# The two halves of a product bank taken in turn, matmul by matmul, in every chunk of a two-layer block

## The chip, the core and the metric

The kernel runs on one core of one Trainium2 chip. The metric is the device time in microseconds of one execution; it stands as the median of several executions. TensorE is PE in the profile (its weight loads are PEld), VectorE is DVE, ScalarE is ACT, GpSimd is POOL, SyncE is SP.

## The reference

A two-layer block on 256 tokens of width 1024, all in float32. What matters here are its large products; each is `activations @ weights`:

```
z = h @ w_in                                   # values va, vb among the columns
merged = sum_b sigmoid(zg_b + b_gate_b) * (y_b @ w_branch[b])      # 3 branches, 256 -> 1024
y = merged @ w_out
a, g = split(h @ w_up);  y = (gelu(conv(a)) * g) @ w_down          # 1024 -> 2816 -> 1024
q, k, v, g, a_lr = split(x @ gla_w_in);  y = (...) @ gla_w_out     # second layer, gated linear attention
k, v = split(x @ w_kv);  q, gate = x @ swa_w_in;  y = (...) @ swa_w_out
```

Between them stand norms, three kinds of attention over 256 tokens, a chunked linear attention and a dilated window attention.

## The kernel before

**Products in three parts.** Every float32 operand is split into a high part in a faster matmul format (`whi`, `hhi`) and the rest (`wlo`, `hlo`). A product of a 128x128 block of weights with 256 columns is then three matmuls: high by high, low by high, high by low. `three` (lines 1596 to 1598) issues them one after the other into one place in PSUM.

**Chunks.** The weights are cut into 106 chunks, mostly 1024 rows by 256 columns, that run in a fixed order: the input projection (MISC, QA, KA, VA, QB, KB, VB, then twelve gate chunks from ZG), three BRANCH chunks, four WOUT, 22 UP, twelve DOWN, the second layer's GK to GG, GOUT, SK, SV, sixteen SWA, SOUT. SP loads each chunk into one of four `raw` buffers, ACT writes `whi` from it (line 639, `high`), DVE writes `wlo` (line 1052, `low`), each in one of three slots. A slot is free when the chunk three before has been multiplied. The order of ACT's and DVE's instructions is written out by hand: in turn c, with b = c - 1, ACT first splits chunk c + 2 and then drains the result of chunk b.

**Results.** A full chunk fills a PSUM bank of 128x512: 256 columns for the first 128 outputs (half i = 0) and 256 for the next (i = 1). There are three result banks, `res0` to `res2`, used in turn. `bank(r)` makes PE wait, ahead of the next matmul that it issues, until result r - 3 is drained. `product_done` counts finished products; ACT and DVE wait for it.

**How the halves are taken before.** A plain chunk of `fm` already takes its halves in turn (`both_sides`, matmuls on line 1631). A chunk that is broken by attention work ("units", `parts`, `half`), or that waits for its input piece by piece (`ready`), does half i = 0 over all eight k and then half i = 1. So do `fm_first` (for each k the three matmuls of a half, then those of the next), `tm` (VA, VB, GV to GV+3, SV to SV+2: tokens as the stationary side, values as result) and the branch projection.

**The down projection.** A pair of output blocks j takes three chunks, kg = 0, 1, 2 with 8, 8 and 6 blocks k, 132 matmuls in all. Its two halves go to two different banks, results r = 2j and r + 1 of this stage. Within each chunk half 0 runs over all its k, then half 1. ACT drains both (lines 863 and 866: the square, then the scaled copy whose end frees the bank); in that turn it has first split chunk b + 3, which takes the slot of the chunk whose end it drains, and so waits for that end:

```python
for i in range(2):
    ps = bank(r + i) if kg == 0 else res[(r + i) % NB]
```

```python
if DOWN <= b < GK and (b - DOWN) % 3 == 2:
    j = (b - DOWN) // 3
    for i in range(2):
        ps = result(FIRST_RESULT[b] + i)
        nc.scalar.activation(sq[:, 2 * j + i, :], ps[:, 0:T], ACT.Square).then_inc(squares["n4"], 1)
```

**Turned.** After the waits at the start of WOUT and UP, `turned` issues three matmuls with the activations as moving and stationary side exchanged into a place that nobody reads.

Of the kernel before, what the change touches and what calls it, by code (L numbers as in the profile page):

```python
# [18 lines left out]
D, T, P = 1024, 256, 128  # L19
KT = D // P  # L20
D_FF = 2816
FT = D_FF // P
# [3 lines left out]
RAW, SPL, NB = 4, 3, 3  # L26
# [12 lines left out]
QI, KK, QC, MISC, QA, KA, VA, QB, KB, VB = range(10)  # L39
# [171 lines left out]
def build(nc, xT, crow_d, cols_d, ident_d, rope1_d, rope2_d, amask_d, cmask_d, tri_d, dmask_d, sel_d, rel_d, w_a2_d,  # L211
# [4 lines left out]
    with ctx:  # L216
# [32 lines left out]
        with ExitStack() as st:  # L249
# [21 lines left out]
            yhi = sb("yhi", [P, 3, 512], f32r, at=st)  # L271
            ylo = sb("ylo", [P, 3, 512], f32r, at=st)
# [3 lines left out]
        w = sq[:, :, :].rearrange("p a b -> p (a b)").rearrange("p (t n) -> p t n", t=2)  # L276
# [19 lines left out]
        with ExitStack() as st:  # L296
            uhi = sb("uhi", [P, FT, T], f32r, at=st)
            ulo = sb("ulo", [P, FT, T], f32r, at=st)
# [50 lines left out]
        res = [ctx.enter_context(nc.psum_tensor(f"res{i}", [P, 512], f32)) for i in range(NB)]  # L349
# [9 lines left out]
        product_done, drained_act, drained_dve = sem("product_done"), sem("drained_act"), sem("drained_dve")  # L359
# [1231 lines left out]
        def _(pe):  # L1591
            mm = nc.tensor.matmul

            def three(out, ah, al, bh, bl, first, last):

                mm(out, ah, bh, start=first, stop=False)  # L1596
                mm(out, al, bh, start=False, stop=False)  # L1597
                return mm(out, ah, bl, start=False, stop=last)  # L1598

            def bank(r):  # L1600

                if r >= DIRECT + NB:
                    who, n = RESULT_DRAIN[r - NB]
                    pe.wait_ge(drained[who], n)
                return res[r % NB]
# [8 lines left out]
            def weights_of(c):  # L1614
                kt, w = kt_of(c)
                return tuple(h[:, 0:kt * w].rearrange("p (k n) -> p k n", k=kt) for h in halves(c))

            def half_product(c, i, k, ps, ih, il, at, first=None, last=None):

                wh, wl = weights_of(c)  # L1620
                return three(ps[:, i * T:i * T + T], wh[:, k, i * P:i * P + P], wl[:, k, i * P:i * P + P],
                             ih[:, k, :], il[:, k, :], at == 0 if first is None else first,
                             at == KT - 1 if last is None else last)

            def both_sides(c, ih, il, ps, order):

                wh, wl = weights_of(c)
                for at, k in enumerate(order):
                    for wt, ix, p in ((wh, ih, 0), (wl, ih, 1), (wh, il, 2)):
                        for i in range(2):  # L1630
                            last = mm(ps[:, i * T:i * T + T], wt[:, k, i * P:i * P + P], ix[:, k, :],  # L1631
                                      start=at == 0 and p == 0 and i == 0, stop=at == KT - 1 and p == 2 and i == 1)
                last.then_inc(product_done, 1)

            def fm(c, ih, il, half=None, ready=None, order=range(KT), parts={}):

                wait_weights(c)
                ps = bank(FIRST_RESULT[c])
                if not half and not ready and not parts:
                    both_sides(c, ih, il, ps, order)  # L1640
                    return
                for i in range(2):
                    for at, k in enumerate(order):
                        if ready and i == 0:
                            ready(k)
                        last = half_product(c, i, k, ps, ih, il, at)
                        if at == 7 and i:
                            last.then_inc(product_done, 1)
                        if at in (3, 7) and 2 * i + at // 4 + 1 in parts:
                            parts[2 * i + at // 4 + 1]()  # L1650
                    if i == 0 and half:
                        half()

            def warm(n, of=ident, to=pS[:, 512:640]):
# [9 lines left out]
            def fm_first(c, ih, il, ready, order=range(KT)):  # L1664


                wait_weights(c)
                wait_weights(c + 1)
                ps = bank(FIRST_RESULT[c]), bank(FIRST_RESULT[c + 1])
                for at, k in enumerate(order):  # L1670
                    ready(k)
                    for d in range(2):
                        for i in range(2):
                            last = half_product(c + d, i, k, ps[d], ih, il, at, i == 0 and at == 0, i == 1 and at == KT - 1)
                        if at == KT - 1:
                            last.then_inc(product_done, 1)

# [9 lines left out]
            def tm(c, ih, il):  # L1687

                wh, wl = weights(c)
                w = kt_of(c)[1]  # L1690
                ps = bank(FIRST_RESULT[c])
                for t in range(2):
                    if c == VB and t == 1:
                        forget_rows((2, 3))
                    for k in range(KT):
                        last = three(ps[:, t * 256:t * 256 + w], ih[:, k, t * P:t * P + P], il[:, k, t * P:t * P + P],
                                     wh[:, k, :], wl[:, k, :], k == 0, k == KT - 1)
                last.then_inc(product_done, 1)

            def in_low(n, k):  # L1700
# [173 lines left out]
            for c in range(DIRECT, NC):  # L1874
# [27 lines left out]
                elif c < WOUT:  # L1902
# [3 lines left out]
                        pe.wait_ge(y_lo, 3)  # L1906
                    for j in range(4):
                        ps = bank(FIRST_RESULT[c] + j)
                        for i in range(2):
                            n = 2 * j + i  # L1910
                            for k in range(2):
                                last = three(ps[:, i * T:i * T + T], wh[:, k, n * P:n * P + P], wl[:, k, n * P:n * P + P],
                                             yhi[:, b, k * T:k * T + T], ylo[:, b, k * T:k * T + T], k == 0, k == 1)
                        last.then_inc(product_done, 1)
                        if (b, j) in ((0, 1), (0, 3), (1, 1)):
                            units((24, 25, 26)[2 * b + j // 2])
# [26 lines left out]
                elif c < GK:  # L1943
# [1 line left out]
                    wh, wl = weights(c)  # L1945
                    kt = kt_of(c)[0]
                    r = 2 * j + FIRST_RESULT[DOWN]
                    for i in range(2):
                        ps = bank(r + i) if kg == 0 else res[(r + i) % NB]
                        for k in range(kt):  # L1950
                            kk = 8 * kg + k
                            if j == 0 and i == 0 and kk % 2 == 0:
                                pe.wait_ge(u_lo, kk // 2 + 1)
                            last = three(ps[:, 0:T], wh[:, k, i * P:i * P + P], wl[:, k, i * P:i * P + P],
                                         uhi[:, kk, :], ulo[:, kk, :], kk == 0, kk == FT - 1)
                        if i == 1 or kg == 2:
                            last.then_inc(product_done, 1)
                    if c == GK - 1:
                        sums("n4", stat)
                        last_squares("n4", stat)  # L1960
# [207 lines left out]
```

## Time and profile before

| | |
|---|---|
| median of 3 executions | 753.88 us |
| lowest, highest | 751.53, 757.02 us |
| the profiled execution | 751.74 us |
| its span, first to last instruction | 749.9 us |
| PE busy | 723.9 us, 5964 matmuls |
| DVE, ACT, POOL busy | 524.3, 395.7, 104.4 us |
| mean granted TensorE clock | 0.989 |

The profiled execution's time is 1.8 us more than its span, and 2.1 us less than the median. A row of a group gives the line, the engine, the instruction, output<-inputs, the number of instructions, and durations. A matmul's duration is modelled and runs past the start of the next, so the rate of PE is read from starts, not from durations.

### The profile page before, as it was taken

Reading aid. Unit: us, or ns where it says so; the run is one execution under the profiler, and the core shown is the slowest. Engines: PE = TensorE matmul, PEld = TensorE weight load, DVE = VectorE, ACT = ScalarE, POOL = GpSimd, SP = SyncE. Lnnn points to the kernel's source line nnn. Section 1 sums busy time; section 2 is a strip of 40 time slices with the busy share of each in tenths; the row PEclk is TensorE's granted clock in tenths of the full one; section 3 lists DMA queues with packets and bytes.
Section 4 is the critical chain, followed back from the end, with each engine's and each line's share of the span. In section 5 each row is a group of like instructions: output and inputs, shape, how many; then the busy total and the mean of one; then the engine's idle time right before and its main releaser. Section 6 shows DMA issues by size and latency. Waiting matters only on the chain.

```text
span 749.9 us, 14222 instructions
## 1 busy us (share of the span) xinstructions
PE 723.9 (97%) x5964; PEld 703.3 (94%) x5964; DVE 524.3 (70%) x778; ACT 395.7 (53%) x560; POOL 104.4 (14%) x87
## 2 busy tenths in 40 slices
PE   8999999998899999999999999999999999999995
PEld 6799899897898999999999989899999999999995
DVE  4979878886978687778776657836576356555665
ACT  4297455555354545544544348537554465556551
POOL 0030000000521000000000130000004465443000
PEclk9999999999999999999999999889999999999999
DMA  8995576566364456565567453604446654333101
GB/s 345 411 361 177 216 278 245 190 240 225 113 225 169 143 195 210 188 221 164 205 267 275 165 199 129 210 25 170 169 155 225 204 191 131 126 138 113 57 1 57
DMA packets 22265, 141.13 MB, mean 188 GB/s; under 512 B 2389, under 2 KB 3029, under 8 KB 6458
## 3 DMA queue, kind: packets, MB, share of 16 engines
q1 hardware_dynamic: 21626, 137.28, 50.4%
q0 software_dynamic: 576, 2.95, 1.0%
q8 instruction: 47, 0.77, 0.4%
q14 instruction: 16, 0.13, 0.0%
HBM read 139.17 MB, written 1.05 MB: 187 GB/s over the span
## 4 chain that ended last, share of the span: by engine, by line
PE 71%; DVE 13%; issue 7%; ACT 6%; DMA 2%; POOL 1%; DVEq 0%; ACTq 0%; POOLq 0%
PE res L1631 22%; PE res L1596 12%; PE res L1598 12%; PE res L1597 12%; ACT whi L639 4%; DVE wlo L1052 3%; PE pX L1816 2%; PE pX L1995 2%; PE pS L1796 1%; DMA shared<-in_w_ada 1%; DVE raw L1065 1%; PE pS L1657 1%; ACT sq L654 1%; DVE shared L1065 1%; PE pT L1806 1%
## 5 line engine op out<-in xcount | busy, mean ns | idle before, releaser
L1052 DVE TENSOR_TENSOR wlo<-raw,whi 128x2048 fp32r<-128x2048 f32 (+3 forms) x101 | 226.9, 2250 | 119.2 <-ACT whi L639 112.7
L639 ACT ACTIVATE whi<-raw 128x2048 fp32r<-128x2048 f32 (+3 forms) x101 | 188.2, 1865 | 102.0 <-issue 73.3
L1596 PE MATMUL res<-hhi,whi 128*128 128x256 f32 (+1 forms) x576 | 166.1, 288 | 4.1 <-DVE wlo L1052 1.5
L1597 PE MATMUL res<-hhi,wlo 128*128 128x256 f32 (+1 forms) x576 | 161.0, 280 | 0.0
L1598 PE MATMUL res<-hlo,whi 128*128 128x256 f32 (+1 forms) x576 | 161.0, 279 | 0.0
L1596 PEld LDWEIGHTS res<-hhi,whi 128*128 128x128 f32 (+1 forms) x576 | 107.5, 187 | 5.9 <-issue 3.4
L1597 PEld LDWEIGHTS res<-hhi,wlo 128*128 128x128 f32 (+1 forms) x576 | 107.5, 187 | 0.3
L1598 PEld LDWEIGHTS res<-hlo,whi 128*128 128x128 f32 (+1 forms) x576 | 107.2, 186 | 0.2
L1631 PE MATMUL res<-hhi,whi 128*128 128x256 f32 x544 | 106.8, 278 | 0.0
L1631 PE MATMUL res<-hlo,whi 128*128 128x256 f32 x544 | 106.4, 277 | 0.0
L1631 PE MATMUL res<-hhi,wlo 128*128 128x256 f32 x544 | 106.3, 277 | 0.0
L1631 PEld LDWEIGHTS res<-hhi,whi 128*128 128x128 f32 x544 | 82.3, 188 | 0.1
L1631 PEld LDWEIGHTS res<-hlo,whi 128*128 128x128 f32 x544 | 82.2, 188 | 0.0
L1631 PEld LDWEIGHTS res<-hhi,wlo 128*128 128x128 f32 x544 | 82.1, 188 | 0.0
L538 POOL TENSOR_TENSOR sq<-sq,rope 128x512 f32<-128x512 f32 x18 | 39.7, 2204 | 77.0 <-ACT sq L654 77.0
L1598 PE MATMUL res<-ulo,whi 128*128 128x256 f32 x176 | 48.6, 276 | 0.0
L1596 PE MATMUL res<-uhi,whi 128*128 128x256 f32 x176 | 48.6, 276 | 0.0
L1597 PE MATMUL res<-uhi,wlo 128*128 128x256 f32 x176 | 48.6, 276 | 0.0
L1065 DVE CUSTOM_DVE_ANT_0 raw<-raw,cact,cols 128x1024 f32<-128x1024 f32 x32 | 41.9, 1346 | 0.0
L1596 PE MATMUL res<-whi,hhi 128*128 128x256 f32 x144 | 40.4, 281 | 0.0
L1597 PE MATMUL res<-whi,hlo 128*128 128x256 f32 x144 | 40.0, 278 | 0.0
L1598 PE MATMUL res<-wlo,hhi 128*128 128x256 f32 x144 | 40.0, 278 | 0.0
(340 smaller groups left out, 1344.4 us busy)
## 6 DMA issues: line engine op xcount, KB each, us to landing
raw<-in_wts SPq DMA_DIRECT2D x97, 1024.0 KB, 4.9
raw<-in_w_ada SPq DMA_DIRECT2D x16, 1024.0 KB, 5.2
shared<-in_w_ada SPq DMA_DIRECT2D x6, 1024.0 KB, 11.0
gates<-in_wts SPq DMA_DIRECT2D x4, 768.0 KB, 13.1
raw<-in_wts SPq DMA_DIRECT2D x4, 768.0 KB, 6.0
y<-in_w_ada SPq DMA_DIRECT2D x2, 1024.0 KB, 9.3
x<-in_xT SPq DMA_DIRECT2D x2, 512.0 KB, 4.5
gv<-in_ln_rows POOLq DMA_DIRECT2D x1, 1024.0 KB, 7.4
```

Of the source, the lines that this page charges most:

```text
L538: nc.gpsimd.tensor_tensor(xsw, xsw, table[:, 1:2, :].to_broadcast([P, 2, T]), ALU.mult).then_inc(sin_done, 1)
L639: nc.scalar.activation(hi[:, 0:kt * w], raw[RAW_OF["w", c] % RAW][:, 0:kt * w], ACT.Copy).then_inc(hi_ready, 1)
L654: nc.scalar.activation(swapped(c)[a:a + block_rows, :, :].rearrange("p a b -> p (a b)"), ps[b:b + block_rows, :], ACT.Copy).then_inc(moved ...
L1052: nc.vector.tensor_tensor(lo[:, 0:b], raw[RAW_OF["w", c] % RAW][:, 0:b], hi[:, 0:b].bitcast(f32), ALU.subtract).then_inc(lo_ready, 1)
L1065: nc.vector.tensor_tensor_reduce(out=w[:, D * i:D * i + D], in0=w[:, D * i:D * i + D], in1=cact[:, :], op0=ALU.mult, op1=ALU.add, scale=1. ...
L1596: mm(out, ah, bh, start=first, stop=False)
L1597: mm(out, al, bh, start=False, stop=False)
L1598: return mm(out, ah, bl, start=False, stop=last)
L1631: last = mm(ps[:, i * T:i * T + T], wt[:, k, i * P:i * P + P], ix[:, k, :], start=at == 0 and p == 0 and i == 0, stop=at == KT - 1 and p = ...
L1657: mm(to, of[:, :], of[:, :], start=True, stop=True)
L1816: last = mm(pX[:, T + P * t:T + P * t + P], v, dpT[:, t, P * i:P * i + P], start=i == 0, stop=i == 3)
L1995: last = mm(pX[po:po + n, P * h + 64 * (ch // 2) + 16 * i:P * h + 64 * (ch // 2) + 16 * i + 16], ekI[:, EK[i] + m * n:EK[i] + m * n + n], ...
```

## The change

A helper `six` takes two outputs and two stationary sides and issues the three parts for both in turn, six matmuls for each k. Everything that went through `half_product`, `tm`, the branch projection and the down projection now uses it. Number, shapes and operands of the matmuls stay; the attention work is put in after the same number of matmuls as before. Where the two halves share a bank, only the first matmul of the bank has `start`. In the down projection both banks are asked for at the start of kg = 0, and the last block k is done with `three` for half 0 and then for half 1, each with its own `product_done`.

```diff
-            def half_product(c, i, k, ps, ih, il, at, first=None, last=None):
+            def six(outs, sides, bh, bl, first, last):
+
+                for p in range(3):
+                    for i, (out, side) in enumerate(zip(outs, sides)):
+                        done = mm(out, side[p % 2], bl if p == 2 else bh, start=first[i] and p == 0, stop=last[i] and p == 2)
+                return done
+
+            def chunk_step(c, k, ps, ih, il, at):
 
                 wh, wl = weights_of(c)
-                return three(ps[:, i * T:i * T + T], wh[:, k, i * P:i * P + P], wl[:, k, i * P:i * P + P],
-                             ih[:, k, :], il[:, k, :], at == 0 if first is None else first,
-                             at == KT - 1 if last is None else last)
+                return six([ps[:, i * T:i * T + T] for i in range(2)],
+                           [(wh[:, k, i * P:i * P + P], wl[:, k, i * P:i * P + P]) for i in range(2)],
+                           ih[:, k, :], il[:, k, :], (at == 0, False), (False, at == KT - 1))
...
                 ps = bank(FIRST_RESULT[c])
-                if not half and not ready and not parts:
-                    both_sides(c, ih, il, ps, order)
-                    return
-                for i in range(2):
-                    for at, k in enumerate(order):
-                        if ready and i == 0:
-                            ready(k)
-                        last = half_product(c, i, k, ps, ih, il, at)
-                        if at == 7 and i:
-                            last.then_inc(product_done, 1)
-                        if at in (3, 7) and 2 * i + at // 4 + 1 in parts:
-                            parts[2 * i + at // 4 + 1]()
-                    if i == 0 and half:
+                for at, k in enumerate(order):
+                    if ready:
+                        ready(k)
+                    last = chunk_step(c, k, ps, ih, il, at)
+                    if at == KT - 1:
+                        last.then_inc(product_done, 1)
+                    if at % 2 and at // 2 + 1 in parts:
+                        parts[at // 2 + 1]()
+                    if at == 3 and half:
                         half()
...
-                for t in range(2):
-                    if c == VB and t == 1:
+                for k in range(KT):
+                    if c == VB and k == KT // 2:
                         forget_rows((2, 3))
-                    for k in range(KT):
-                        last = three(ps[:, t * 256:t * 256 + w], ih[:, k, t * P:t * P + P], il[:, k, t * P:t * P + P],
-                                     wh[:, k, :], wl[:, k, :], k == 0, k == KT - 1)
+                    last = six([ps[:, t * 256:t * 256 + w] for t in range(2)],
+                               [(ih[:, k, t * P:t * P + P], il[:, k, t * P:t * P + P]) for t in range(2)],
+                               wh[:, k, :], wl[:, k, :], (k == 0, False), (False, k == KT - 1))
...
-                    for i in range(2):
-                        ps = bank(r + i) if kg == 0 else res[(r + i) % NB]
-                        for k in range(kt):
-                            kk = 8 * kg + k
-                            if j == 0 and i == 0 and kk % 2 == 0:
-                                pe.wait_ge(u_lo, kk // 2 + 1)
-                            last = three(ps[:, 0:T], wh[:, k, i * P:i * P + P], wl[:, k, i * P:i * P + P],
-                                         uhi[:, kk, :], ulo[:, kk, :], kk == 0, kk == FT - 1)
-                        if i == 1 or kg == 2:
-                            last.then_inc(product_done, 1)
+                    outs = [(bank(r + i) if kg == 0 else res[(r + i) % NB])[:, 0:T] for i in range(2)]
+                    for k in range(kt):
+                        kk = 8 * kg + k
+                        if j == 0 and kk % 2 == 0:
+                            pe.wait_ge(u_lo, kk // 2 + 1)
+                        if kk == FT - 1:
+                            for i in range(2):
+                                three(outs[i], wh[:, k, i * P:i * P + P], wl[:, k, i * P:i * P + P],
+                                      uhi[:, kk, :], ulo[:, kk, :], False, True).then_inc(product_done, 1)
+                        else:
+                            last = six(outs, [(wh[:, k, i * P:i * P + P], wl[:, k, i * P:i * P + P]) for i in range(2)],
+                                       uhi[:, kk, :], ulo[:, kk, :], (kk == 0, kk == 0), (False, False))
+                    if kg < 2:
+                        last.then_inc(product_done, 1)
```

The branch projection is changed like `tm`: for each of its two k the two output blocks of a bank go through `six`.

## Rows read from the trace of the kernel before

**Rows 1.** The page: busy shares, granted clock in 40 slices, the chain by engine.

```profile
PE 723.9 (97%) x5964; PEld 703.3 (94%) x5964; DVE 524.3 (70%) x778; ACT 395.7 (53%) x560; POOL 104.4 (14%) x87
...
PEclk9999999999999999999999999889999999999999
...
PE 71%; DVE 13%; issue 7%; ACT 6%; DMA 2%; POOL 1%; DVEq 0%; ACTq 0%; POOLq 0%
```

**Rows 2.** One line's matmuls in a stretch, halves in turn: UP, then GG+2 and GG+3.

```profile
L1631 PE MATMUL res<-hhi,whi x320: 276/276/277, 251.1 to 359.3; 128*128 128x256 f32 x160
...
L1631 PE MATMUL res<-hhi,whi x32: 279/280/280, 513.5 to 524.3; 128*128 128x256 f32 x32
```

**Rows 3.** The same view, half after half: gate chunk, tm twice, DOWN, SWA.

```profile
L1596 PE MATMUL res<-hhi,whi x8: 276/276/363, 143.2 to 145.7; 128*128 128x256 f32 x8
...
L1596 PE MATMUL res<-whi,hhi x48: 281/281/283, 455.2 to 471.8; 128*128 128x256 f32 x48
...
L1596 PE MATMUL res<-whi,hhi x48: 276/276/282, 576.0 to 592.0; 128*128 128x256 f32 x48
...
L1596 PE MATMUL res<-uhi,whi x176: 276/276/276, 359.9 to 419.4; 128*128 128x256 f32 x176
...
L1596 PE MATMUL res<-hhi,whi x12: 279/279/362, 622.1 to 626.1; 128*128 128x256 f32 x12
```

**Rows 4.** The same view of KA, a plain chunk right after attention work.

```profile
L1631 PE MATMUL res<-hhi,whi x16: 279/280/365, 52.1 to 57.2; 128*128 128x256 f32 x16
```

**Rows 5.** Timeline before DOWN and at its first pair's end: start us, us, engine, what.

```profile
357.23 0.57 ACT L849 ACTIVATE aseq<-res 128x512 f32<-128x512 f32 x1
...
374.86 0.28 PE L1596 MATMUL res<-uhi,whi 128*128 128x256 f32 x1
...
375.11 1.49 ACT L639 ACTIVATE whi<-raw 128x1536 fp32r<-128x1536 f32 x1 [1.72 <-issue]
...
376.50 0.37 ACT L863 ACTIVATE sq<-res 128x256 f32<-128x256 f32 x1
...
376.76 0.47 ACT L866 ACTIVATE y<-res,pcol 128x256 f32<-128x256 f32 x1
...
377.58 0.28 PE L1596 MATMUL res<-uhi,whi 128*128 128x256 f32 x1
```

**Rows 6.** Timeline at the ends of the second and the third pair.

```profile
389.82 0.28 PE L1596 MATMUL res<-uhi,whi 128*128 128x256 f32 x1
...
391.73 0.46 ACT L866 ACTIVATE y<-res,pcol 128x256 f32<-128x256 f32 x1
...
404.78 0.28 PE L1596 MATMUL res<-uhi,whi 128*128 128x256 f32 x1
...
406.69 0.47 ACT L866 ACTIVATE y<-res,pcol 128x256 f32<-128x256 f32 x1
```

**Rows 7.** Timeline where PE resumes after a wait for ACT, in the branch projection.

```profile
179.32 0.82 ACT L779 ACTIVATE gates<-res,bgh 128x256 f32<-128x256 f32 x2
...
180.19 0.39 PE L1596 MATMUL res<-yhi,whi 128*128 128x256 f32 x1 [1.89 <-ACT gates L779]
...
180.41 0.28 PE L1597 MATMUL res<-yhi,wlo 128*128 128x256 f32 x1
```

**Rows 8.** Timeline at the end of DOWN, where the norm's sums follow.

```profile
419.74 1.02 PE L1718 MATMUL pX<-sq,meanw 128*128 128x256 f32 x4
419.94 0.38 ACT L863 ACTIVATE sq<-res 128x256 f32<-128x256 f32 x1 [1.29 <-PE res L1598]
...
420.22 0.47 ACT L866 ACTIVATE y<-res,pcol 128x256 f32<-128x256 f32 x1
...
420.60 1.03 PE L1724 MATMUL pX<-sq,meanw 128*128 128x256 f32 x4
```

**Rows 9.** Stretches: us, PE busy (matmuls), granted clock, DMA share, GB/s.

```profile
480.60:494.10 13.50, 13.50 (x136) 0.50 0.44 157
176.00:183.00 7.00, 4.54 (x36) 1.00 0.57 172
```

**Rows 10.** Timeline of three product matmuls at the low clock.

```profile
493.43 0.41 PE L1596 MATMUL res<-hhi,whi 128*128 128x256 f32 x1
493.64 0.41 PE L1597 MATMUL res<-hhi,wlo 128*128 128x256 f32 x1
493.85 0.41 PE L1598 MATMUL res<-hlo,whi 128*128 128x256 f32 x1
```

More of the change, by code:

```diff
@@ L1616, in weights_of @@
                 return tuple(h[:, 0:kt * w].rearrange("p (k n) -> p k n", k=kt) for h in halves(c))
-            def half_product(c, i, k, ps, ih, il, at, first=None, last=None):
-                wh, wl = weights_of(c)
-                return three(ps[:, i * T:i * T + T], wh[:, k, i * P:i * P + P], wl[:, k, i * P:i * P + P],
-                             ih[:, k, :], il[:, k, :], at == 0 if first is None else first,
-                             at == KT - 1 if last is None else last)
-            def both_sides(c, ih, il, ps, order):
-                wh, wl = weights_of(c)
-                for at, k in enumerate(order):
-                    for wt, ix, p in ((wh, ih, 0), (wl, ih, 1), (wh, il, 2)):
-                        for i in range(2):
-                            last = mm(ps[:, i * T:i * T + T], wt[:, k, i * P:i * P + P], ix[:, k, :],
-                                      start=at == 0 and p == 0 and i == 0, stop=at == KT - 1 and p == 2 and i == 1)
-                last.then_inc(product_done, 1)
+            def six(outs, sides, bh, bl, first, last):
[4 more added lines that the diff above has]
+            def chunk_step(c, k, ps, ih, il, at):
+                wh, wl = weights_of(c)
+                return six([ps[:, i * T:i * T + T] for i in range(2)],
+                           [(wh[:, k, i * P:i * P + P], wl[:, k, i * P:i * P + P]) for i in range(2)],
+                           ih[:, k, :], il[:, k, :], (at == 0, False), (False, at == KT - 1))
             def fm(c, ih, il, half=None, ready=None, order=range(KT), parts={}):
@@ L1638, in fm @@
                 ps = bank(FIRST_RESULT[c])
-                if not half and not ready and not parts:
-                    both_sides(c, ih, il, ps, order)
-                    return
-                for i in range(2):
-                    for at, k in enumerate(order):
-                        if ready and i == 0:
-                            ready(k)
-                        last = half_product(c, i, k, ps, ih, il, at)
-                        if at == 7 and i:
-                            last.then_inc(product_done, 1)
-                        if at in (3, 7) and 2 * i + at // 4 + 1 in parts:
-                            parts[2 * i + at // 4 + 1]()
-                    if i == 0 and half:
+                for at, k in enumerate(order):
[7 more added lines that the diff above has]
+                    if at == 3 and half:
                         half()
@@ L1672, in fm_first @@
                     for d in range(2):
-                        for i in range(2):
-                            last = half_product(c + d, i, k, ps[d], ih, il, at, i == 0 and at == 0, i == 1 and at == KT - 1)
+                        last = chunk_step(c + d, k, ps[d], ih, il, at)
                         if at == KT - 1:
@@ L1908, in _ @@
                         ps = bank(FIRST_RESULT[c] + j)
[L1909 to L1913, printed above, removed]
+                        for k in range(2):
+                            last = six([ps[:, i * T:i * T + T] for i in range(2)],
+                                       [(wh[:, k, n * P:n * P + P], wl[:, k, n * P:n * P + P]) for n in (2 * j, 2 * j + 1)],
+                                       yhi[:, b, k * T:k * T + T], ylo[:, b, k * T:k * T + T], (k == 0, False), (False, k == 1))
                         last.then_inc(product_done, 1)
@@ L1947, in _ @@
                     r = 2 * j + FIRST_RESULT[DOWN]
-                    for i in range(2):
-                        ps = bank(r + i) if kg == 0 else res[(r + i) % NB]
-                        for k in range(kt):
-                            kk = 8 * kg + k
-                            if j == 0 and i == 0 and kk % 2 == 0:
-                                pe.wait_ge(u_lo, kk // 2 + 1)
-                            last = three(ps[:, 0:T], wh[:, k, i * P:i * P + P], wl[:, k, i * P:i * P + P],
-                                         uhi[:, kk, :], ulo[:, kk, :], kk == 0, kk == FT - 1)
-                        if i == 1 or kg == 2:
-                            last.then_inc(product_done, 1)
+                    outs = [(bank(r + i) if kg == 0 else res[(r + i) % NB])[:, 0:T] for i in range(2)]
[12 more added lines that the diff above has]
+                        last.then_inc(product_done, 1)
                     if c == GK - 1:
```

## The prediction

> **What bounds the kernel now.** I read the page first: PE is busy for 723.9 of 749.9 us and carries 71% of the chain, DVE 13%, ACT 6% [rows 1]. The kernel is bound by PE's stream of matmuls, so a change of their order matters in two ways: it can change the pace at which they start, and it can change what PE has to wait for. The clock is full but for a dip in slices 26 and 27. The second reading is therefore of pace, from the view of one line's matmuls in a stretch, by first and last start; the third is the timeline at the places where the new order asks for something earlier or gives something later.
>
> **The pace, and whether the order sets it.** In UP, halves in turn, the high-by-high matmuls stand in pairs: from 251.1 to 359.3 us lie 159 times six matmuls and one, 955, so 108.2 / 955 = 113.3 ns from start to start [rows 2]. In DOWN, half after half, it is 59.5 us over 175 times three, 113.3 ns as well [rows 3]. So there, taking the halves in turn or not gives the same pace to a tenth of a nanosecond, and 113.3 ns is what PE does at best on this shape. But there is a second pace. GG+2 and GG+3, halves in turn, take 10.8 us over 91 matmuls, 118.7 ns (rounding of the times is 1 ns of it) [rows 2]; the first three GV chunks, `tm`, 16.6 us over 141, 117.7 ns, while the SV chunks, the same code, take 16.0 us over 141, 113.5 ns [rows 3]. The two paces go with modelled durations of 276 and of 279 to 281 ns, which makes each stretch easy to sort: a gate chunk's half at 276, an SWA stretch at 279 [rows 3], KA, in turn, at 279 to 280 [rows 4]. Both orders run at both paces. The slower one appears almost always when PE comes to the product from small attention matmuls, and holds until something switches it. The order of the halves is not what tells them apart in any row, so I cost the new order itself at nothing in the 2,784 matmuls that it touches (560 triples of `fm` and `fm_first`, 144 of `tm`, 176 of DOWN, 48 of the branch projection, counted in the code; MISC, GA, GOUT and SOUT stay).
>
> Bounds of that nothing: of the 1,680 matmuls of `fm` and `fm_first`, all but about 130 stand at the slower pace (the exceptions are five stretches of 24 and one of 12; [rows 3] has one), and 144 of `tm` do; so 1,690 times 4.5 ns (117.8 less 113.3), 7.6 us, is the most that these can give. The branch projection's 144 stand at about 120 ns and could give 1 us, and 192 unchanged matmuls that inherit the pace (GG+2, GG+3, SK+1, SK+2) 0.9 us: 9.5 us in all. On the other side UP's 960 matmuls and DOWN's 528 stand at the good pace and could lose 1,488 times 4.5 ns, 6.7 us. I take zero because KA, in turn and straight after attention matmuls, is at the slower pace [rows 4], as are the other two plain chunks in such a place.
>
> **Where a product is broken or waits.** The attention work comes after the same number of matmuls (12 or 24), a full chunk ends after 48, so its drain, the slot for the next weights and the score matmuls stand where they stood: zero, and no queue is passed. The waits by k (`ready`, u_lo in the first pair of DOWN) are reached later than before, since each k now has six matmuls ahead of the next in place of three: no loss, and no gain either, for PE does not stand at them now outside `fm_first`, whose order by k is the same.
>
> **DOWN: a wait that did not bind before.** This is the term that counts. The two halves go to two banks, and kg = 0 now asks for both at once. Half 1 of pair j needs the bank that half 0 of pair j - 1 filled (r + 1 - 3 = r - 2). Before, PE asked for it 24 matmuls into the pair. The first pair ends and the second begins at 374.86; half 1's first matmul starts at 377.58 [rows 5]. ACT frees that bank with the scaled copy at 376.76 + 0.47 = 377.23 us, just 0.35 us ahead. It can't do so sooner: its program has the split of the next chunk but two first (375.11, 1.49 us), which waits for the end of the pair itself, then the square (376.50), then the copy. That half 0's product was done 18 matmuls earlier never helped it, and doesn't now. So after the change PE stands at the pair's start until that copy ends. From an ACT end to PE's first matmul it is 0.05 us (179.32 + 0.82 = 180.14, matmul at 180.19) and the first matmul after such a wait is followed by the next in 0.22 us where 0.113 would do: 0.11 us more [rows 7]. The stall is thus
> - pair 1: 377.23 + 0.05 - 374.86 + 0.11 = 2.53 us [rows 5, 7];
> - pair 2: 391.73 + 0.46 + 0.05 - 389.82 + 0.11 = 2.53 us [rows 6];
> - pair 3: 406.69 + 0.47 + 0.05 - 404.78 + 0.11 = 2.54 us [rows 6].
>
> Together 7.6 us. The first pair starts at 359.9 [rows 3]; the later of its two banks was UP's last but one result, which ACT had copied out by 357.8 [rows 5]: no stall. Behind PE's waiting instruction is only PE's own stream; ACT, DVE and the weight loads are prefetching and follow it at the same distance, so nothing gives the 7.6 us back: PE's stream is the chain before and after.
>
> **The end of DOWN.** Half 0 of the last pair is now done three matmuls before half 1 instead of 18. ACT's four steps close up: square 0 at about 419.60, copy 0 at 419.86, square 1 at 420.22 (it was 419.94), by the distances 0.26 and 0.36 us that the same steps have in [rows 5, 8]. PE's second pair of sums begins at 420.60 and needs square 0 first and square 1 only half of 0.86 us later [rows 8]; square 1 ends at 420.60. Hidden by PE's own sums, and 0.3 us if I misread that.
>
> **The sum.** 751.74 + 7.6 = 759.3 us for an execution like the profiled one, whose span would be 757.5. The median of the runs is 2.1 us above the profiled execution, so the forecast is 753.88 + 7.6 = 761.5 us.
>
> **Rivals.**
> - *The pace gets worse too.* After each of the three stalls PE resumes and may take up the slower pace: 396 matmuls times 4.5 ns = 1.8 us, 763.3. Or the switch back that `turned` makes in UP fails, and all of UP and DOWN run at 118: 6.7 us, 768.2. For it: after attention work the slower pace is the rule. Against: in the trace a wait in mid-product leaves the pace that was there.
> - *Taking halves in turn is itself the cure.* If it brings the good pace wherever attention work breaks a product, 9.5 us come back and the stalls are more than paid: 761.5 - 9.5 = 752.0, not slower than before. It decides against me from 7.6 us, that is if some 1,690 matmuls gain 4.5 ns each. For it: the long stretch at the best pace in UP is in turn. Against: GG+2, GG+3 and KA are in turn and slow [rows 2, 4], DOWN is not and fast [rows 3].
> - *No stall, no new pace*: ACT reaches the copy sooner than its order says, or PE is held less long; 753.9. The order of ACT's instructions speaks against it. If it went with the cure of the pace: 744.4, the only way to faster.
> - *The clock falls in the stalls.* The clock went down to 0.50 once, for 13.5 us from 480.6, after a stretch of tiny matmuls, and did not in the branch projection, where PE was busy for 4.54 of 7 us and stood still for 1.9 us at a time [rows 7, 9]. A fall per stall at that length would cost 13.5 x (1 - 0.113 / 0.21), since matmuls of this shape start 0.21 us apart there [rows 10]: 6.2 us, 19 in all, 780.
>
> The Trainium skill ("TensorE: Matmul & The Clock Gate", HAM oscillation) says that waits between bursts of matmuls can throttle the array again, and so speaks against this change. The 1.9 us wait of this trace does not show it; a 2.4 us one is not in the trace.
>
> **How the numbers follow.** Forecast (stalls as worked out, pace as it is, small shifts of single stretches either way, 760 to 763.5): 0.50. Worse pace: 0.20. Cure of the pace, whole or in part (752 to 758): 0.14. No stall: 0.08. Clock: 0.03. Both good things: 0.05. The range leaves out the clock, the faster case and the lower end of the cure, and reaches 768 above and 753.5 below. Within 1%, about what a measurement of this kernel can tell from no change, ends at 761.4, in the middle of my forecast's case: slower by over 1% is half of it, the worse pace and the clock, 0.50; faster by over 1% 0.05; the rest 0.45.
>
> **What would show it.** In the trace after: PE idle of about 2.4 us three times at the start of kg = 0 in DOWN, released by ACT's scaled copy on line 866 or where that stands; DOWN from first to last start 59.8 + 7.6 us; UP at 113.3 ns; SWA and gate stretches with durations of 279 ns; the sums after DOWN back to back. I am wrong if those three waits are not there, if the median duration in the gate and SWA stretches is 276, or if UP or DOWN shows 279.

## The result, and the profile after

The changed kernel took 766.23 us (median of four executions, 760.96 to 768.31) against 755.45 us of the kernel before in the same comparison; the ratio is 1.0121, with a 95% interval from 1.0067 to 1.0176. Slower, by 1.2%; the interval lies wholly between 1 and 1.02. Forecast had been 761.5 us. There are only four executions of each kernel here, and the kernel before turns out to have two groups of times, so the size is less sure than the sign: the two medians lie 10.8 us apart, the ratio stands for 9.1 us.

The profiled execution took 768.31 us, its span 766.5 us, 16.6 us more than before. The page, its busy shares, its clock and its chain, against [rows 1]:

```profile
PE 731.9 (95%) x5964; PEld 710.9 (93%) x5964; DVE 524.8 (68%) x778; ACT 396.3 (52%) x560; POOL 104.4 (14%) x87
...
PEclk9999999999999999999999999969999999999999
...
PE 36%; DVE 5%; issue 3%; ACT 1%; POOL 0%; DVEq 0%; ACTq 0%
```

The same 5964 matmuls, but PE is busy for 8 us more and idle for 8.6 us more. (The chain covers only part of the span here, so nothing below rests on it.) What PE waited for, from the view of waits (total us, times, longest), opens with a line that the kernel before does not have:

```profile
PE res L1622 <- ACT y L866: 7.1, 3, 2.4
```

At the end of DOWN's first pair the timeline shows it, where [rows 5] had PE running on:

```profile
380.16 0.28 PE L1598 MATMUL res<-ulo,whi 128*128 128x256 f32 x1
...
380.52 1.49 ACT L639 ACTIVATE whi<-raw 128x1536 fp32r<-128x1536 f32 x1 [2.32 <-DVE wlo L1052]
...
381.91 0.37 ACT L863 ACTIVATE sq<-res 128x256 f32<-128x256 f32 x1
382.18 0.47 ACT L866 ACTIVATE y<-res,pcol 128x256 f32<-128x256 f32 x1
...
382.79 0.48 PE L1622 MATMUL res<-uhi,whi 128*128 128x256 f32 x2 [2.35 <-ACT y L866]
```

Split, square, copy, and PE 0.14 us behind the copy's end: 2.63 us from the last matmul's start to the next one's, against 0.113. The other two waits are as long: 2.5 us more than a normal step each. Two further things are in the trace. First the clock, from the view of stretches (length us, PE busy and matmuls, granted clock, DMA share, GB/s). The first row is the whole first pair, with no wait ahead of it; the others are the 48 matmuls that open the next three (the view also counts a matmul or two that reach over an edge):

```profile
364.73:380.30 15.57, 15.57 (x134) 1.00 0.57 206
382.79:390.05 7.26, 7.26 (x49) 0.76 0.86 318
402.45:408.18 5.73, 5.73 (x48) 1.00 0.77 292
420.59:427.85 7.26, 7.26 (x48) 0.76 0.82 292
```

After the first and the third wait the clock fell to 0.50 for a while: 7.26 in place of 5.73 us, 1.53 us lost each time. Second, the pace, by which the distance from one matmul's start to the next's is meant. The same line's matmuls in UP and DOWN, which [rows 2, 3] had at 276:

```profile
L1622 PE MATMUL res<-hhi,whi x320: 279/280/282, 251.7 to 364.1; 128*128 128x256 f32 x160
...
L1622 PE MATMUL res<-uhi,whi x168: 279/279/416, 364.7 to 436.5; 128*128 128x256 f32 x168
```

The whole of UP and DOWN ran at 117.8 ns from start to start. And in the SWA stretches it was the other way round, 276 where [rows 3] had 279:

```profile
L1622 PE MATMUL res<-hhi,whi x12: 276/276/363, 646.7 to 650.3; 128*128 128x256 f32 x12
```

The 16.6 us by stage, from first starts: UP begins 1.0 us later (a shift of the first stages, whose cause I did not look for); `fm_first` of UP was at the good pace and gave 0.4 back; UP's plain chunks cost 4.3 us; DOWN, from its first to its last start, 72.90 in place of 59.73 us, costs 13.2 (three waits 7.5, slow first steps 0.3, two falls of the clock 3.1, pace 528 x 4.5 ns = 2.4); then 0.4 us around the long stretch at the low clock that both profiles have ([rows 9]); and SWA gives back 1.8. The open question was which of these belong to the change and which to the execution.

### The profile page after: what moved, and what is told of

It is laid out like the page before. It is cut to its first block and busy times, and to the rows that moved or that the text cites. A ratio compares the mean times of both kernels' runs of the same rounds, so it can differ in the third digit from the quotient of the medians.

```text
span 766.5 us, 14223 instructions
## 1 busy us (share of the span) xinstructions
PE 731.9 (95%) x5964; PEld 710.9 (93%) x5964; DVE 524.8 (68%) x778; ACT 396.3 (52%) x560; POOL 104.4 (14%) x87
## 5 line engine op out<-in xcount | busy, mean ns | idle before, releaser
L1622 PE MATMUL res<-hhi,whi 128*128 128x256 f32 x1104 | 224.0, 284 | 4.1 <-DVE wlo L1052 1.6
L1622 PE MATMUL res<-hhi,wlo 128*128 128x256 f32 x1104 | 218.7, 279 | 0.0
L1622 PE MATMUL res<-hlo,whi 128*128 128x256 f32 x1104 | 218.4, 279 | 0.0
L1622 PEld LDWEIGHTS res<-hhi,whi 128*128 128x128 f32 x1104 | 168.9, 189 | 5.9 <-issue 3.4
L1622 PEld LDWEIGHTS res<-hlo,whi 128*128 128x128 f32 x1104 | 168.6, 188 | 0.0
L1622 PEld LDWEIGHTS res<-hhi,wlo 128*128 128x128 f32 x1104 | 168.5, 188 | 0.0
L1622 PE MATMUL res<-uhi,wlo 128*128 128x256 f32 x168 | 34.6, 288 | 0.0
L1622 PE MATMUL res<-ulo,whi 128*128 128x256 f32 x168 | 34.5, 288 | 0.0
L1622 PEld LDWEIGHTS res<-uhi,whi 128*128 128x128 f32 x168 | 27.0, 197 | 7.6 <-issue 7.6
L1622 PEld LDWEIGHTS res<-uhi,wlo 128*128 128x128 f32 x168 | 26.9, 197 | 0.0
## 6 DMA issues: line engine op xcount, KB each, us to landing
gates<-in_wts SPq DMA_DIRECT2D x4, 768.0 KB, 13.2
raw<-in_wts SPq DMA_DIRECT2D x4, 768.0 KB, 5.4
```

Of the source, the lines that this page charges most:

```text
L1622: done = mm(out, side[p % 2], bl if p == 2 else bh, start=first[i] and p == 0, stop=last[i] and p == 2)
```

## The experiments

In what follows "low group" is an execution at 750 to 756 us or, with stalls, its counterpart, and "high group" one some 7 us above. "Fall" is a fall of the clock to half. In the nine profiles of kernels that do not wait in DOWN the groups are the pace of UP and DOWN: the six executions at 751 to 755 us have them at 113.3 ns, the three at 759 to 761 at 117.8.

**Both kernels once more.** No edit. The kernel before:

> The kernel before, once more, to see whether the pace of a stretch (113.3 or 117.8 ns between starts) belongs to the program or to the execution. If to the program: UP's plain chunks and DOWN at 113.3 again, the SWA stretches at 117.8, span within 1 us of 749.9. If to the execution: some long stretch stands at the other pace; UP and DOWN at 117.8 would make the span about 756.6.

It took 752.62 us, span 750.8; UP and DOWN at 113.3. Only small stretches had changed sides (SK was fast, SV slow). The changed kernel:

> The changed kernel once more. The three stalls of 2.4 us at the pairs of DOWN must be there in either theory. If the pace belongs to the program: UP and DOWN at 117.8 and SWA at 113.3 as in its first profile, span near 766.5. If to the execution: UP and DOWN may stand at 113.3, and then the span is 766.5 less 6.7, about 760, which fits the spread of its four times from 761.0 to 768.3.

It took 761.06 us, span 759.3, and this time UP's plain chunks stood at the good pace:

```profile
L1622 PE MATMUL res<-hhi,whi x320: 276/276/280, 250.8 to 359.4; 128*128 128x256 f32 x160
```

The three waits are there, 7.1 us in all. So the pace of UP belongs to the execution. The two spans of the changed kernel lie 7.2 us apart: UP's pace is 3.8 of it (plain chunks 4.3, `fm_first` -0.4), DOWN's 1.6 (its second pair and the start of its third ran at 117.8 here, the rest at 113.3), and most of the rest the long stretch at the low clock, 10.2 us here and 13.7 in the first profile. SWA was at 113.3 in this profile too; on that below.

**DOWN as before, all else in turn.** The down projection's loop is put back (`for i in range(2): ps = bank(r + i) ...`, half after half).

> The changed kernel with the down projection as before, all else in turn. My theory (the loss is DOWN's wait for its second bank, order itself costs nothing): ratio to before 1.00, 0.995 to 1.005, no wait of PE at the pairs of DOWN. Rival (halves in turn in the other chunks give back some of it): 0.987 to 0.995. Rival (they upset the pace of UP): 1.005 to 1.01.

Ratio 1.0018 (0.9977 to 1.006), no wait of PE on line 866. Its twelve times fall into two groups with nothing between: five at 751.4 to 752.8, seven at 758.1 to 760.3. The kernel before shows the same two groups, 11 of 17 executions in this comparison at 751.2 to 754.6 and 6 at 757.9 to 760.9. Its profile, an execution of 752.6 us, had UP and DOWN at 113.3, and SWA, in turn as in the changed kernel, at the slow pace:

```profile
L1622 PE MATMUL res<-hhi,whi x12: 279/280/365, 629.4 to 633.2; 128*128 128x256 f32 x12
```

**DOWN alone in turn**, the rest as before.

> The kernel before with the down projection alone in turn. My theory: three waits of 2.4 us, ratio 1.010 (7.6 us), up to 1.015 where the clock also falls after a wait, as it did for about 3.4 us after two of three in the changed kernel's profile. If the loss came from UP's pace in the changed kernel instead: 1.000 to 1.005 here, UP at 113.3.

Ratio 1.0181 (1.0134 to 1.0229), times from 764.6 to 771.4. The profile has the three waits (7.1 us), one fall in DOWN, and UP and DOWN at 117.8. The ratio is above the 1.010 to 1.015 that I had expected: in this comparison 11 of 17 executions of the kernel before were in the low group, while the profile here had UP at the slow pace. DOWN alone costs all that the change costs, or a little more; nothing that the change did elsewhere is needed to explain the loss.

**DOWN's first chunk half after half, the rest in turn.** This takes the reason of the wait away and leaves two thirds of DOWN in turn:

```diff
+                    if kg == 0:
+                        for i in range(2):
+                            ps = bank(r + i)
+                            for k in range(kt):
...
+                                last = three(ps[:, 0:T], wh[:, k, i * P:i * P + P], wl[:, k, i * P:i * P + P],
+                                             uhi[:, k, :], ulo[:, k, :], k == 0, False)
+                        last.then_inc(product_done, 1)
+                    else:
+                        outs = [res[(r + i) % NB][:, 0:T] for i in range(2)]
```

> The changed kernel, but in DOWN's first chunk of each pair half 0 runs before half 1, so that the second bank is asked for 24 matmuls later, as before; the other two chunks are in turn, and the last block finishes as in the change. My theory: no wait of PE on the scaled copy, DOWN 59.8 us at the good pace, ratio 1.00 (0.995 to 1.006, by how often UP stands at the slow pace). Rival (in DOWN the order itself, or the late end of half 0, costs time): a wait stays or DOWN is over 61 us at the good pace, ratio 1.008 or more.

Ratio 0.998 (0.9941 to 1.0019), eight of twelve in the low group. The row of the first chunks (and of each pair's last block, which stands on the same line) is back where [rows 3] had it, and the wait on line 866 is gone:

```profile
L1596 PE MATMUL res<-uhi,whi x72: 276/276/276, 360.9 to 420.4; 128*128 128x256 f32 x72
```

DOWN took 59.73 us from first to last start, as in the kernel before. So what cost time in DOWN was the moment at which the second bank is asked for, neither the order nor the late end of half 0.

**ACT drains first.** The changed kernel, with ACT's split of the next chunk but two moved behind the drains of the pair:

```diff
-                if b not in LATE and b not in (GOUT + 1, GOUT + 2) and b != WOUT + 2 and b >= DIRECT:
+                if b not in LATE and b not in (GOUT + 1, GOUT + 2) and b != WOUT + 2 and b >= DIRECT and not (DOWN <= b < GK and (b - DOWN) % 3 == 2):
                     high(c + 2)
...
                                              scale=pcol[:, 3, 2 * j + i:2 * j + i + 1]).then_inc(drained_act, 1)
+                    if b not in LATE:
+                        high(c + 2)
```

> The changed kernel, but ACT drains the pair's two results before it splits the next chunk but two. My theory: square and copy of half 0 end about 0.75 us after the pair's last matmul, so the wait shrinks from 2.5 to 1.1 us with the slow first step (1.0 us idle), and the clock doesn't fall after it: 3.4 us in place of 7.6 and of the clock's share, ratio 1.003 to 1.008. Rival (the wait comes from elsewhere, a late weight split or DVE): waits of 2.4 us as before, or new ones at kg = 2, where the chunk split later is used; ratio 1.01 or more.

Ratio 1.0042 (1.0002 to 1.0082), times from 754.45 to 764.68. The waits shrank from 2.51 to 0.75 us beyond the normal distance, 1.7 us in all by the view of waits, and none was followed by a fall:

```profile
377.62 0.38 ACT L863 ACTIVATE sq<-res 128x256 f32<-128x256 f32 x1 [1.34 <-PE res L1600]
377.64 0.28 PE L1600 MATMUL res<-ulo,whi 128*128 128x256 f32 x1
377.90 0.47 ACT L866 ACTIVATE y<-res,pcol 128x256 f32<-128x256 f32 x1
...
378.51 0.47 PE L1624 MATMUL res<-uhi,whi 128*128 128x256 f32 x2 [0.59 <-ACT y L866]
```

They are shorter by 1.8 us. The split is 1.4 of it (1.49 us, 0.1 of which the square overlapped). The other 0.4 is ACT's start: its first step now needs only half 0, which ends three matmuls sooner, and so the square starts just ahead of the pair's last matmul, where the split started 0.36 us behind it. I had expected 1.1 us with the slow first step; 0.83 was measured.

The profile also shows what a wait can do to the pace. The first pair of DOWN (41 of its matmuls), ahead of any wait, and the three pairs behind the first wait:

```profile
L1624 PE MATMUL res<-uhi,whi x41: 276/276/276, 362.8 to 376.4; 128*128 128x256 f32 x41
...
L1624 PE MATMUL res<-uhi,wlo x126: 279/280/282, 378.8 to 425.8; 128*128 128x256 f32 x126
```

From 113.3 to 117.8 at the first wait, and slow to the end through two more: 1.8 us of this kernel's DOWN (63.94 us; 59.73 + 2.2 of waits + 0.2 of first steps + 1.8).

**The kernel before without the turned matmuls ahead of UP.** The two lines that call `turned` at UP + 2 are left out; nobody reads their result.

> The kernel before without the three turned matmuls ahead of UP's plain chunks. If the pace is carried on from matmul to matmul and the turned ones switch it: UP's plain chunks and DOWN mostly at 117.8, the pace of the chunks ahead of them, and most executions at 758 to 761 where most were at 751 to 755. If the pace belongs to the order or to the chunks: UP at 113.3, times as before less 0.3 us.

Inconclusive as a test of timing: three of ten in the low group, ratio 0.9997 (0.9957 to 1.0038), with 11 of 35 in it for the kernel before beside it. The profile speaks to the mechanism. It caught an execution in which `fm_first` of UP was fast already, and without the turned ones the pace was carried on, 113.3 to the end of DOWN; in the changed kernel's first profile `fm_first` was fast too and UP was slow behind the turned triple.

**A fixed start ahead of UP.** One float32 matmul and six turned ones in place of three:

```diff
                         if c == UP + 2:
+                            wait_weights(c)
+                            warm(1)
+                            turned(c)
                             turned(c)
```

> The kernel before, but ahead of UP's plain chunks stand one float32 matmul with the identity and six turned matmuls, the sequence in which VA begins; VA was at the good pace in all six traces so far. If such a start sets the pace whatever it was: UP and DOWN at 113.3 in every execution, no times at 758 to 761, highest under 756, median near 753, ratio about 0.997. If it only flips the pace like the single turned triple: times in two groups as before.

My forecast of its sign was wrong and its use was greater for it. All twelve executions are in the high group, 758.55 to 762.06, median 760.23: this start sets the pace, to the slow one. It puts two things in at once, the float32 matmul and a second turned triple; which of them does it no run separates. The kernel before beside it had 11 of 35 in the low group. UP in the profile:

```profile
L1631 PE MATMUL res<-hhi,whi x318: 278/279/280, 252.7 to 364.5; 128*128 128x256 f32 x159
```

With the pace pinned, which each execution otherwise draws anew as in a lottery, the orders can be compared on equal terms. The same start in the changed kernel, and in the kernel with DOWN as before:

> The changed kernel with the float32 matmul and six turned matmuls ahead of UP's plain chunks, which pinned the kernel before to the slow pace (twelve executions, 758.6 to 762.1, median 760.2). If the order of the halves is worth nothing and the stalls in DOWN are the loss: UP and DOWN at 117.8 in the profile, waits of 2.4 us, and times that stand 7.6 to 11 us above 760.2 (one to two falls of the clock), less up to 2.4 where SWA is at the good pace: 766 to 771, with no time under 765. If halves in turn give the good pace after such a start: UP at 113.3, times near 761.

> The same start in the kernel in which everything but DOWN takes its halves in turn. With the pace of UP pinned, the order alone is left. My theory: median 760.2 within 0.8 us, all times in one group from 758 to 762. Rival (in turn is better or worse by itself outside DOWN): median under 758.5 or over 762.

Measured side by side, the first took 769.21 to 772.34 us (four executions, median 769.80), the second 757.94 to 761.33 (twelve, median 759.65). The halves in turn outside DOWN are thus worth 759.65 - 760.23 = -0.6 us at this pace (from two comparisons on different chips, so no more than "about nothing"), and DOWN's new order costs 769.80 - 759.65 = 10.2 us. The spans of the two profiles, 768.0 and 757.8 us, differ by 10.2 too, 9.3 of it in DOWN (71.36 and 62.07 us): three waits 7.5, first steps 0.2, one fall 1.5. The other 0.9 is what is left of 1.0 us less ahead of UP and 1.8 more behind DOWN, so that the two 10.2 agree so well is luck.

**A start that should give the good pace.** Ahead of UP's plain chunks one float32 matmul, six with the weights as the stationary side, then the turned triple:

```diff
+                            wh, wl = weights(c)
+                            warm(1)
+                            for k in range(2):
+                                three(pS[:, 512:768], wh[:, k, 0:P], wl[:, k, 0:P], hhi[:, k, :], hlo[:, k, :], True, True)
                             turned(c)
```

> The kernel before, but ahead of UP's plain chunks stand one float32 matmul, six matmuls with the weights as the stationary side, and the three turned ones. In the traces so far a start after float32 matmuls is nearly always slow (95 in 100), and the turned triple switched slow to fast in 13 of 16 cases, fast to slow in one of one. If so: UP and DOWN at 113.3 in most executions, ten of twelve at 751 to 756, median 753.5. If the pace after the turned ones is chance or depends on more: two groups as before.

(Over the ten profiles of that moment, the triples ahead of WOUT's and UP's plain chunks came after the slow pace 17 times and were followed by the fast one 15 times; once it was the other way round. If a triple mostly flips the pace, two in a row behind a float32 matmul would end slow, as they did above. No run tests that by itself.) Nine of twelve executions are in the low group, median 754.14 us, against 758.39 of the kernel before beside it, with 11 of 23 in it. The ratio of 0.9988 (0.995 to 1.0027) does not tell that from no change.

**All that helped, together**: this start, and DOWN's first chunk half after half, in the changed kernel.

> All that helped, together: the changed kernel with DOWN's first chunk half after half (no wait for the second bank) and the start of the last experiment ahead of UP (one float32 matmul, six with weights stationary, three turned). Expected: UP and DOWN at 113.3, no wait on the scaled copy, nine or more of twelve executions at 752 to 755.5, median 754, 0 to 5 us under the kernel before's median in the same call, 10 or more under the changed kernel. Rival (in turn outside DOWN does upset UP's pace): two groups of equal size, median 757 or more.

Nine of twelve again, median 753.16 us against 759.61, ratio 0.9955 (0.9918 to 0.9992): the only version whose interval lies under 1, by less than half a per cent. Within the low group it is no faster than the kernel before (751.6 to 755.1 against 752.0 to 753.4): it was in that group more often. Its profile happens to be one of the three slow executions (760.52 us): UP's `fm_first` was slow, and UP stayed slow behind the new start. The start does not fix the pace. Over both kernels with it 6 of 24 executions are in the high group, where the kernel before has 24 of 40 beside them and 54 of 92 in all comparisons together. That the start improves the odds is likely, not shown: without it, the kernel with DOWN's first chunk half after half had 4 of 12 in the high group.

## Why the prediction was right or wrong

**The forecast as a whole: the mechanism it rests on took place, the number came in with help.** The 766.2 us are 4.7 above the 761.5 and fall inside the stated range by its room for a worse pace, outside the 760 to 763.5 of the case that was forecast. Of the signs of being wrong that it named, the 279 ns in UP and DOWN appeared in the first profile, and the 276 ns in SWA, though not in the gate stretches; the three waits were there as said. (Its 0.50 for slower by over 1% adds up to 0.48.) The 768.2 us of the rival with all of UP and DOWN slow and the 768.3 of the profiled execution agree by luck: that execution also had two falls (3.1 us), 1.0 us more ahead of UP and 1.8 less in SWA.

**DOWN's stalls: right in place, cause and number, undersized in what follows them.** Forecast were three waits of 2.53 us, slow first step included, 7.6 in all; measured are three of 2.51 us and 0.08 more for the first step (PE came 0.14 us behind the copy, not 0.05). Doing DOWN alone brings the whole loss, moving the request for the bank takes all of it away, and moving ACT's split of 1.49 us out of the way shortens each wait by 1.8. That chain of causes is shown.

**"The clock falls in the stalls", 0.03, was far too low in chance and four times too high in price.** Falls followed 6 of the 12 waits of 2.5 us in the four profiles that have them (two, two, one and one of three), each within 0.5 to 1.5 us of PE's return, and 0 of the 3 waits of 0.75 us; DOWN has no fall in the nine profiles without waits. Each cost 1.53 us, not 6.2: I had taken the length of the one long fall in the middle of the trace, which had another stretch of PE ahead of it. I leaned on the branch projection, where PE waits for 1.9 us amid smaller work and the clock had held. It holds there only in some executions; the profile of the kernel with DOWN as before has this:

```profile
181.00:183.60 2.60, 2.60 (x15) 0.50 0.38 57
```

It did so in 8 of all 14 profiles, so one trace that shows no fall was weak evidence. The Trainium skill ("TensorE: Matmul & The Clock Gate", HAM oscillation) says that waits between bursts of matmuls can throttle the array again; the waits of its own example last 3 to 5 us. These rows agree, and show it for waits of 2.5 us, and of 1.9 us in the branch projection.

**"The order costs nothing by itself": right.** With UP's pace pinned the medians with and without it over the 2,256 matmuls outside DOWN differ by 0.6 us; and in DOWN the in-turn chunks of the third experiment ran at 113.3.

**"In mid-product a wait leaves the pace that was there": nearly always.** Of the 15 waits in DOWN only the first one of the kernel that drains first clearly changed it, from fast to slow, which cost 1.8 us. In the second profile of the changed kernel the pace changed twice, but where the clock fell. Behind its second wait (397.8 us) it stayed slow until the clock fell at 399.1, and it was fast when the clock came back at 402.5:

```profile
L1622 PE MATMUL res<-uhi,wlo x4: 278/279/280, 398.1 to 398.9; 128*128 128x256 f32 x4
...
L1622 PE MATMUL res<-uhi,wlo x32: 276/276/276, 403.1 to 413.4; 128*128 128x256 f32 x32
```

Behind its first wait PE made two steps at 113 to 114 ns before the clock fell, too few to be sure of, and was slow when it came back. In the other four falls of DOWN the pace was slow before and after. So the reason given in the rival "the pace gets worse too", that PE may take up the slower pace after a stall, held once. What that rival priced at 768.2, all of UP and DOWN slow, is what the first profile shows, but UP was slow there before DOWN began.

**UP's pace: I priced it right (6.7 us) and took it for a property of the program.** It changes from one execution to the next in the kernel before as well, and splits nearly all its times into 751 to 755 and 757.5 to 762. The three executions known when I forecast were mostly low ones, so "753.88 + 7.6" had a base that later medians put at 754 to 760. Of the 16.6 us between the two first profiles, 6.3 (UP's 4.3 - 0.4 and DOWN's 2.4) is this lottery and not the change.

**The cure of the pace.** It had 0.14, and none came that can be put down to the order. Ahead of the branch projection, where attention work breaks most chunks, the median duration is 279 ns in all 14 profiles, in either order. The profiles of all in-turn kernels but the changed one itself have SWA at 117.8; the changed kernel had it at 113.3 twice in two, worth 1.8 us in the first. Why that program and not its neighbours was not settled.

**The sum.** The change costs 9.3 to 11.5 us in DOWN by the pinned and the second profile, and 10.2 us by times; the ratio of 1.0121 says 9.1. The forecast 7.6 lacked about one and a half falls of the clock (2.3 us), the mean of the four profiles.

## What to carry to other kernels

When outputs that used to be made one after the other are made together, look at when each buffer is asked for, not only at how many there are: here a bank was free 0.35 us before its use, and asking for it 2.7 us earlier turned that into a wait of 2.5 us for an engine whose program puts a step of 1.49 us ahead of the drain. Price a new wait as the wait and what follows it: here a fall of the clock in 6 of 12, and now and then another pace behind the wait or behind the fall. And take two or three traces of the same kernel before a pace or a clock is called its property; two groups of times are a sign that something is decided anew in each execution, and pinning it, even to the bad side, allows the comparison that noise had hidden.

## What the runs showed of the hardware

- A stream of these matmuls (128x128 stationary, 256 columns) keeps one of two paces, 113.3 or 117.8 ns from start to start, for up to 1,488 matmuls on end (UP's plain chunks and DOWN in the kernel before), through changes of chunk, bank and order. The modelled durations (276, 279 to 281 ns) tell them apart.
- The changes of pace that were found stand where float32 matmuls, a wait, a fall of the clock or an exchange of the stationary and the moving side comes in, and not each of these changes it: 1 of the 15 waits in DOWN clearly did, 1 or 2 of the 6 falls there, 16 of 18 turned triples. The same instructions can come out either way in different executions; a float32 matmul followed by six turned ones came out slow in the three profiles that have it, and by their times in all 28 executions of three kernels. What decides was not found.
- The clock can fall to half after a single wait of 2.5 us amid dense matmuls: it did in 6 of 12 cases, and cost 1.53 us each time. Behind the branch projection's wait of 1.9 us, with less dense work around it, it did in 8 of 14 profiles.
